# Last mixer: projections of two heads at a time in quarters, with attention units, rotation and head norm of the group ahead of them between

## The reference, cut to what matters

```python
def diff_attn_mixer(h, w_in, lam_vecs, subln_w, w_out, cos, sin, layer):
    y = h @ w_in
    q, k, v = jnp.split(y, 3, axis=-1)
    q = apply_rope(q.reshape(B, L, DIFF_HEADS, 2, DIFF_HEAD), cos, sin)
    k = apply_rope(k.reshape(B, L, DIFF_HEADS, 2, DIFF_HEAD), cos, sin)
    v = v.reshape(B, L, DIFF_HEADS, 2 * DIFF_HEAD)
    lam = jnp.exp(jnp.sum(lv[0] * lv[1])) - jnp.exp(jnp.sum(lv[2] * lv[3])) + lam_init
    o = causal_diff_attention(q, k, v, lam)   # (softmax of component 0 - lam * softmax of component 1) @ v
    o = rmsnorm(o, subln_w, SUBLN_EPS) * (1.0 - lam_init)   # within each head
    return o.reshape(B, L, D_MODEL).astype(h.dtype) @ w_out
```

## Time and profile before

| | us |
|---|---|
| median of 3 runs | 1783.93 |
| lowest and highest | 1777.27, 1785.84 |
| the profiled execution | 1785.98 |
| its span | 1784.2 |

### The profile page before, as it was taken

One profiled execution on the slowest core, in us unless ns is written; L12 is line 12 of the kernel. 1 busy time (PEld: TensorE's weight loads), 2 busy tenths in 40 slices (PEclk: granted clock), 3 DMA queues, 4 the chain that ended last, 5 costly groups with the idle time before them and its releaser, 6 DMA issues. The chain is left out here.

```text
span 1784.2 us, 33804 instructions
## 1 busy us (share of the span) xinstructions
PE 1622.2 (91%) x14218; PEld 1542.3 (86%) x14218; DVE 1036.1 (58%) x1581; ACT 739.4 (41%) x1025; POOL 75.8 (4%) x98
## 2 busy tenths in 40 slices
PE   2999989989998889999789997899998979799997
PEld 2999979989997889999688987899998956689997
DVE  6999466887655665444685524544335365655443
ACT  2554344872215444443450103465333434456432
POOL 0121000001100001100000000000000030000000
PEclk7999989999999999999899976999999985799998
DMA  9898545432113546555330002254442510235451
GB/s 352 293 349 342 195 139 195 166 119 90 61 49 112 189 154 247 186 168 188 107 100 27 2 1 78 88 177 157 170 170 103 168 32 1 95 102 185 164 186 48
DMA packets 39195, 256.77 MB, mean 144 GB/s; under 512 B 4259, under 2 KB 5668, under 8 KB 9892
## 3 DMA queue, kind: packets, MB, share of 16 engines
q1 hardware_dynamic: 37492, 251.07, 40.3%
q10 hardware_dynamic: 1584, 3.97, 0.6%
HBM read 251.87 MB, written 3.15 MB: 143 GB/s over the span
## 5 line engine op out<-in xcount | busy, mean ns | idle before, releaser
L454 DVE TENSOR_TENSOR w_lo<-raw,w_hi 128x2048 fp32r<-128x2048 f32 (+2 forms) x203 | 456.6, 2249 | 474.3 <-ACT w_hi L446 473.5
L528 PE MATMUL bank<-x_hi,w_hi 128*128 128x256 f32 (+1 forms) x2096 | 609.3, 291 | 56.6 <-DVE x_lo L677 28.6
L529 PE MATMUL bank<-x_lo,w_hi 128*128 128x256 f32 (+1 forms) x2096 | 600.0, 286 | 0.0
L530 PE MATMUL bank<-x_hi,w_lo 128*128 128x256 f32 (+1 forms) x2096 | 599.5, 286 | 0.0
L446 ACT ACTIVATE w_hi<-raw 128x2048 fp32r<-128x2048 f32 (+2 forms) x203 | 381.6, 1880 | 422.7 <-PE bank L530 399.6
L528 PEld LDWEIGHTS bank<-x_hi,w_hi 128*128 128x128 f32 x2096 | 401.1, 191 | 67.4 <-issue 53.0
L530 PEld LDWEIGHTS bank<-x_hi,w_lo 128*128 128x128 f32 x2096 | 401.9, 192 | 0.0
L529 PEld LDWEIGHTS bank<-x_lo,w_hi 128*128 128x128 f32 x2096 | 400.4, 191 | 1.0 <-issue 0.7
L528 PE MATMUL bank<-mh_hi,w_hi 128*128 128x272 f32 (+1 forms) x512 | 149.0, 291 | 6.5 <-PEq L2666 6.5
L530 PE MATMUL bank<-mh_hi,w_lo 128*128 128x272 f32 (+1 forms) x512 | 147.7, 289 | 0.0
L529 PE MATMUL bank<-mh_lo,w_hi 128*128 128x272 f32 (+1 forms) x512 | 147.0, 287 | 0.0
(11 more groups left out here) (489 smaller groups left out, 2203.5 us busy)
## 6 DMA issues: line engine op xcount, KB each, us to landing
raw<-in_stream SPq DMA_DIRECT2D x227, 1024.0 KB, 4.8
raw<-in_stream SPq DMA_DIRECT2D x8, 768.0 KB, 4.3
gate_store<-stage ACTq DMA_DIRECT2D x8, 256.0 KB, 2.0
raw<-in_stream SPq DMA_DIRECT2D x4, 512.0 KB, 3.8
h<-in_h ACTq DMA_DIRECT2D x1, 1088.0 KB, 8.2
zt<-gate_store SPq DMA_DIRECT2D x1, 1024.0 KB, 6.5
gate<-gate_store SPq DMA_DIRECT2D x1, 1024.0 KB, 8.6
out<-h SPq DMA_DIRECT2D x8, 128.0 KB, 1.9
```

Source lines behind the costliest of these rows:

```text
L454: nc.vector.tensor_tensor(w_lo[:, s_at % 2, 0:kt], raw[:, r_at % RING, 0:kt], w_hi[:, s_at % 2, 0:kt].bitcast(F32), ALU.subtract).then_inc ...
L528: nc.tensor.matmul(out, hi, xh[:, k0 + k, 0:L], start=start, stop=False)
L529: nc.tensor.matmul(out, hi, xl[:, k0 + k, 0:L], start=False, stop=False)
L530: mm = nc.tensor.matmul(out, lo, xh[:, k0 + k, 0:L], start=False, stop=stop)
```

## The change

The twelve slabs of q, k and v are ordered by groups of two heads: q, k, v of heads 0 and 1, then of 2 and 3, and so on, each slab a section of its own. Blocks 1 to 5 become one block, whose engines walk 26 slots (s from -4 to 21). In slots -4 to 11 PE issues three quarters of a slab in each (a quarter is one half of the columns over four of the eight tiles), so that four slots project a group. Unit s of the attention is issued in slot s, its transposition in s+2, its product with the values in s+3, its head's norm from slot 2h+4 for head h on. While group g is projected, the units of the group before are at work. The last four units have no projections beside them.

The projections accumulate in banks 0 and 1; scores have one pair of banks (2, 3) up to unit 12, the rotation and the transposed values banks 4 and 5, transposed weights bank 6, products with values bank 7. DVE now makes both products of the rotation from the accumulation banks, ahead of the permutation (`turn_products`), and adds the permuted one behind it (`turned`); GpSimd has no part in it. A finished head is copied by ACT. Results of the norm go to `o_hi` and `o_lo` of their own. The block opens with the norm `before_attention`; DVE has ahead of it the first operations for lambda, and SP has `turning` and `lam_row` ahead of the slabs.

```diff
-    add("od_q", 4, by_cols("od_w_in_2", K8), taker="act")
-    add("od_kv", 8, by_cols("od_w_in_2", K8, 0, D), taker="act")
+    for g in range(4):
+        add(f"od_q{g}", 1, by_cols("od_w_in_2", K8, 0, g * SLAB_N))
+        add(f"od_k{g}", 1, by_cols("od_w_in_2", K8, 0, D + g * SLAB_N))
+        add(f"od_v{g}", 1, by_cols("od_w_in_2", K8, 0, 2 * D + g * SLAB_N), taker="act")
...
-        plain(S["od_q"], x_hi[:, :, META:T2], x_lo[:, :, META:T2], q_at, before=before_attention, L=T1)
-        plain(S["od_kv"], x_hi, x_lo, yq)
...
+        GROUPS, UNITS, STREAMED = 4, 2 * HEADS, 12
+        units = [(head, qt) for head in range(HEADS) for qt in range(2)]
+        woven = [S[f"od_{x}{g}"] for g in range(GROUPS) for x in "qkv"] + [S["od_out"]]
+        slots = range(-4, UNITS + 6)
...
+                sp.dma_start(turning[:], t["turning"]).then_inc(a["turn"], 16)
                 sp.dma_start(lam_row[:], t["od_lambda_2"]).then_inc(a["lam"], 16)
-                sp.dma_start(turning[:], t["turning"]).then_inc(a["turn"], 16)
+                load_to(sp, S["od_out"].r0 + 1 + RING)
...
+                def quarter(m):
+                    p, j, k0 = m // 4, m // 2 % 2, 4 * (m % 2)
+                    sec, _, (r, r_at, s, s_at, _) = slab(p)
+                    cols = kept(p % 3)
+                    if m % 4 == 0:
+                        pe.wait_ge(raw_used, r + 1 + RING)
+                        if p == 0:
+                            keep_busy(w_hi[:, s_at % 2, 0, 0:P], w_hi[:, s_at % 2, 1], FIRST_BUSY)
+                    if k0 == 0 and p:
+                        if j:
+                            taken(pe, woven[p - 1], None, 0, 0)
+                        else:
+                            pe.wait_ge(a["half_took"], p)
+                    out = banks[j][:, 0:T2 - cols.start]
+                    for k in range(k0, k0 + 4):
+                        if p == 0 and j == 0:
+                            before_attention.wait_tile(pe, k)
+                        hi = w_hi[:, s_at % 2, k, j * P:(j + 1) * P]
+                        lo = w_lo[:, s_at % 2, k, j * P:(j + 1) * P]
+                        nc.tensor.matmul(out, hi, x_hi[:, k, cols], start=k == 0, stop=False)
+                        nc.tensor.matmul(out, hi, x_lo[:, k, cols], start=False, stop=False)
+                        mm = nc.tensor.matmul(out, lo, x_hi[:, k, cols], start=False, stop=k == 7)
+                    if k0:
+                        mm.then_inc(slab_done if j else a["half_done"], 1)
...
+                def rotated(g, kind):
+                    if g == 0 and kind == 0:
+                        pe.wait_ge(a["turn"], 16)
+                    if kind:
+                        pe.wait_ge(a["rope"], 4 * g + 2)
+                    elif g:
+                        pe.wait_ge(a["v_out"], 2 * g)
+                    n = T2 - kept(kind).start
+                    for j in range(2):
+                        pe.wait_ge(a["by_sin"], 4 * g + 2 * kind + j + 1)
+                        nc.tensor.matmul(banks[4 + j][:, 0:n], rotate, by_sin[:, kind, j, 0:n], start=True, stop=True).then_inc(a["rot"], 1)
+
+                def rows_of_values(g):
+                    half_took = 3 * g + 3
+                    pe.wait_ge(a["rope"], 4 * g + 4)
...
+                def scores(n):
+                    head, qt, C, K = dims(n)
+                    if qt == 0 and head % 2 == 0:
+                        pe.wait_ge(a["rope"], 2 * head + 4)
+                    if n:
+                        pe.wait_ge(u_["exp"], n if n <= STREAMED else n - 1)
+                    if n == STREAMED + 1:
+                        pe.wait_ge(a["v_out"], 2 * GROUPS)
...
+                for s in slots:
+                    first, i, g = 3 * (s + 4), s % 4, s // 4 + 1
+                    if s < STREAMED:
+                        quarter(first)
+                    if 0 <= s < UNITS:
+                        scores(s)
+                    if s >= 5 and s % 2 and (s - 5) // 2 < HEADS:
+                        head_sum((s - 5) // 2)
+                    if s < STREAMED:
+                        quarter(first + 1)
+                    if 0 <= s - 2 < UNITS:
+                        transposed_weights(s - 2)
+                    if s < STREAMED:
+                        quarter(first + 2)
+                    if 0 <= s - 3 < UNITS:
+                        weighted_values(s - 3)
+                    if s < STREAMED and i in (2, 3):
+                        rotated(g, i - 2)
+                    if i == 0 and 0 <= s <= STREAMED:
+                        rows_of_values(s // 4)
...
+                def turn_products(g, kind, j):
+                    p = 3 * g + kind
+                    half_ready(dve, p, j)
+                    if g == 0 and kind == 0 and j == 0:
+                        dve.wait_ge(a["turn"], 16)
+                    if g:
+                        dve.wait_ge(a["rot"], 4 * (g - 1) + 2 * kind + j + 1)
+                    cols = kept(kind)
+                    n = T2 - cols.start
+                    nc.vector.tensor_tensor(by_sin[:, kind, j, 0:n], banks[j][:, 0:n], sin_t[:, cols], ALU.mult).then_inc(a["by_sin"], 1)
+                    nc.vector.tensor_tensor(target(g, kind, j), banks[j][:, 0:n], cos_t[:, cols], ALU.mult).then_inc(dve_took if j else a["half_took"], 1)
...
+                dve.wait_ge(a["lam"], 16)
+                link(dve, "dve", nc.vector.tensor_tensor(lam_p[:], lam_row[:, 0:4:2], lam_row[:, 1:4:2], ALU.mult))
+                nc.vector.reduce_sum(lam_s[:, 0:2], lam_p[:], AX.X).then_inc(a["lam_x"], 1)
+                link(dve, "dve", nc.vector.tensor_scalar(sub_w[:], col("od_subln_w_2", 0), 1.0 - LAM_INIT, None, ALU.mult))
+                before_attention.on_dve(dve, mid_od)
+                split_lo(dve, slab(1))
+                dve.wait_ge(a["lam_e"], 1)
+                link(dve, "dve", nc.vector.tensor_tensor(lam_s[:, 2:3], lam_s[:, 1:2], lam_s[:, 0:1], ALU.subtract))
+                nc.vector.tensor_scalar(lam_s[:, 3:4], lam_s[:, 2:3], -LAM_INIT, None, ALU.add).then_inc(a["lam_x"], 1)
+                for s in slots:
+                    i, g = s % 4, s // 4 + 1
+                    if i == 0 and 0 <= s <= STREAMED:
+                        turned(s // 4, 1)
+                    if s == 0:
+                        dve.wait_ge(a["lam_mm"], 1)
+                        link(dve, "dve", nc.vector.tensor_copy(lam[:], banks[6][:, 0:1]))
+                    if s < STREAMED:
+                        if i == 2:
+                            turn_products(g, 1, 0)
+                        if i == 3:
+                            turned(g, 0)
+                    unit(s)
+                    if s >= 5 and s % 2 and (s - 5) // 2 < HEADS:
+                        mean_square((s - 5) // 2)
+                    if s < STREAMED:
+                        if i == 0:
+                            turn_products(g, 0, 0)
+                        if i == 1:
+                            turn_products(g, 0, 1)
+                        if i == 2:
+                            turn_products(g, 1, 1)
+                        if i and 3 * g + i + 1 < len(woven):
+                            split_lo(dve, slab(3 * g + i + 1))
+                    if s >= 6 and s % 2 == 0 and (s - 6) // 2 < HEADS:
+                        normed((s - 6) // 2)
+                    if s >= 7 and s % 2 and (s - 7) // 2 < HEADS:
+                        low((s - 7) // 2)
...
+                before_attention.on_act(act, mid_od, lambda: split_hi(act, slab(1)))
+                act.wait_ge(a["lam_x"], 1)
+                nc.scalar.activation(lam_s[:, 0:2], lam_s[:, 0:2], ACT.Exp).then_inc(a["lam_e"], 1)
+                for s in slots:
+                    i, g = s % 4, s // 4 + 1
+                    if i == 1 and 1 <= s <= STREAMED + 1:
+                        value_rows(s // 4)
+                    if 0 <= s < UNITS:
+                        exponentials(s)
+                    if s < STREAMED and i == 3:
+                        copy_values(g, 0)
+                    if 0 <= s - 2 < UNITS:
+                        tr_copy(s - 2)
+                    if s < STREAMED and i in (1, 2):
+                        split_next(3 * g + i - 1)
+                    if s >= 4 and s % 2 == 0 and (s - 4) // 2 < HEADS:
+                        head_out((s - 4) // 2)
+                    if s >= 5 and s % 2 and (s - 5) // 2 < HEADS:
+                        root((s - 5) // 2)
+                    if s >= 7 and s % 2 and (s - 7) // 2 < HEADS:
+                        high((s - 7) // 2)
+                    if s < STREAMED and i == 3:
+                        copy_values(g, 1)
+                        split_next(3 * g + 2)
```

More of the change, by code:

```diff
@@ L2649, in mixer_out @@
                 norm, then = Norm(out, L, g_row(layer, 1), add_to=hs), Norm(hs, L, g_row(layer, 2))
-                plain(sec, x_hi, x_lo, out, norm=norm, then=then, L=L)
+                plain(sec, xh, xl, out, norm=norm, then=then, L=L)
             return then
```

(47 more changed lines are left out.)

285 lines of the change are left out of this document (107 added, 178 removed).

## The result

The changed kernel takes 1773.51 us (median of 10 runs, 1772.27 to 1779.31) against 1781.72 for the kernel before in the same comparison (10 runs, 1777.27 to 1785.84). The medians lie 8.2 us apart. The ratio on record is 0.9944, 95% interval 0.9931 to 0.9957, which is some 10 us faster, 7.7 to 12.3.

A forecast was written before the change was run, and what follows sets the result against it. It took 98.5 us without projections as what could be won, and the DVE-ACT split chain as the new limit. Steps of 172.6 us plus 4 gave 176.6 against 179.1, so 1781.4 us; range 1758 to 1797.

The forecast's parts named there:

- 1 opening: Block start to end of first slab: 12.2 us before, plus 3.5 us waiting for lambda behind the tables; 15.7 us.
- 2 two slabs, rotation: After the first slab: two more slabs and one rotation without units, at PE's pace; 13.0 us.
- 3 to scores 1: Value copy, splits, rotated keys, first scores, then PE's list without a unit to finish; 11.7 us.
- 4 scores 1 to 5: First group with units: four slots without norm, root, high and low parts; 33.2 us.
- 5 scores 5 to 9: Second group with units: as a full group of four slots, without one low part; 38.1 us.
- 6 scores 9 to 13: Third group: slot 11 has no split, slot 12 runs at half clock; 32.2 us.
- 7 the rest: Units 13 to 15, then the last unit's attention, its product and the last two heads' norm; 28.7 us.
- The hand-overs: Waits spread over some 80 hand-overs between engines in the block, 0.05 us each; 4 us added.
- PE's own pace: PE's work for a full group at full clock: 28.9 us, 7.2 a slot, against 9.6 expected from the chain.
- A looser chain: Streamed groups near PE's pace, 29 to 33 us each; whole time 1762 to 1774, about 1768; chance 0.35.
- The clock stays at half: PE's waits in the streamed part keep its clock at half; 1826 if throughout, 1797 if partly; chance 0.15.
- Table switches that cost twice their load: Each ScalarE table switch costs another 1.3 us beyond its load; 7 us more, 1788; chance 0.05.

The follow-up runs named there:

- lam_later: Changed kernel with lambda's DMA ahead of the tables' and its DVE operations behind the opening norm; block 167.15 us, 0.9969 of before.
- fill_waits: Changed kernel with useless matmuls on PE ahead of the scores of slots 0, 4, 8 and 12; block 164.73 us, 0.9922 of before.
- splits_slot12: splits_lam with root and high part of the head norm ahead of value copies and high split in slots 3 and 7; block 145.66 us, 1755.16 us.
- splits_slot13: splits_lam with ScalarE's high split of slots 2, 6 and 10 back behind the exponentials; block 151.31 us, 0.9850 of before.
- high_split_first: Changed kernel with ScalarE's high splits ahead of exponentials, or of weight copies, root and high part in fourth slots; block 160.25 us, 0.9891 of before.
- splits_lam: splits_both with lambda's operations also behind the opening norm; block 148.74 us, 0.9830 of before.
- splits_both: Changed kernel with high splits first on ScalarE and each fourth slot's low split behind the next slot's first unit; block 151.56 us, 0.9835 of before.

## Why the prediction came out as it did

The mechanism was right, and so were most terms; one term was added on top that the steps didn't need. Step by step, forecast and measured in the profile of after (the measured steps hold their hand-overs):

| step | forecast us | measured us |
|---|---|---|
| 1 opening | 15.7 | 15.3 (1351.09 to 1366.35) |
| 2 two slabs, rotation | 13.0 | 13.0 |
| 3 to scores 1 | 11.7 | 13.3 |
| 4 scores 1 to 5 | 33.2 | 32.6 |
| 5 scores 5 to 9 | 38.1 | 37.8 |
| 6 scores 9 to 13 | 32.2 | 30.6 |
| 7 the rest | 28.7 | 27.6 |
| hand-overs | 4 | in the steps |
| sum | 176.6 | 170.2 |

- **The hand-overs (4 us) are the step that failed.** I added 80 times 0.05 us to the steps. The price of a unit was read from one start to another start (1478.26 to 1480.90) and held its hand-overs already. The other terms of the chain were mostly durations of single instructions, and in the trace of after these overlap on the same engine by more than the hand-overs take:

```profile
1427.88 0.56 ACT L3051 ACTIVATE attn_tr<-bank 128x128 f32<-128x128 f32 x3
...
1428.35 1.90 ACT L448 ACTIVATE w_hi<-raw 128x2048 fp32r<-128x2048 f32 x1
...
1430.28 2.29 DVE L456 TENSOR_TENSOR w_lo<-raw,w_hi 128x2048 fp32r<-128x2048 f32 x1 [2.06 <-ACT w_hi L448]
...
1432.49 0.43 DVE L2912 TENSOR_TENSOR by_sin<-bank,turning 128x272 f32<-128x272 f32 x1
```

  The split starts 0.09 us before the copy ends and the product 0.08 before the low split ends, against 0.03 us of hand-over from ACT to DVE. From the mask at 1425.23 to this product it is 7.26 us, forecast 2.64 + 0.56 + 1.92 + 2.29 = 7.41. Without the hand-overs the sum is 172.6, 6.5 us faster than before, against 8.9 measured.
- **Opening.** Right in mechanism and size: the norm starts 3.1 us after the block (1354.21), forecast 3.5, and waits for lambda behind the tables. lam_later gives the 3.0 us back.
- **Step 3, 1.6 us short.** The term holds no half clock behind PE's wait. The wait was only 2.47 us, and the clock was at half all the same (0.52 from 1387 to 1390). fill_waits gives back 1.5 us in just this step.
- **Groups 1 and 2.** Within 0.6 us, and by the mechanism named: low splits wait for high splits (27.2 us in 11 places), PE waits 3.84 and 5.14 us at the scores of slots 4 and 8, and the clock is at half behind. I had put these waits at 5 us or more, which only the second is. The slots themselves: masks of units 5 to 9 lie 8.0, 9.1, 11.9 and 8.8 us apart, forecast 7.4 (7.8 without the low part), 9.5, 11.4 and 9.8. The errors, +0.6, -0.4, +0.5 and -1.0, cancel nearly in the sum, which is luck.
- **Group 3 and the rest**, 1.6 and 1.1 us too high. Before the scores of slot 12 PE waited only 2.27 us, and 12 table loads lie in the block, not 16: one for lambda, six for the roots, as the last three roots have no exponentials between them and share one, and five for the exponentials.
- **PE's own pace.** I put a full group of PE's work at 28.9 us. In splits_slot12, where nothing else holds it up, PE is busy for 28.89 us of a second group of 29.4. So the total of PE's list was right. The 8.4 us between this group's 29.4 and after's 37.8 are what the order costs, the half clock included. "PE waits a third of the time" was wrong by its own numbers: 38.5 less 28.9 is a quarter of 38.5, and in the trace PE was idle for 6.5 of 37.8 us.
- **The rivals.** A looser chain, with groups at 29 to 33 us, wasn't the case: 37.8 in the second. That the whole time lies inside its 1762 to 1774 is chance. The clock stays at half: no, it is back at 1.00 by 1390, 1421 and 1459, some 5 to 6 us after PE's work began again at 1384.80, 1416.14 and 1453.31. Table switches that cost twice their load: no, 4.4 us in sum without eleven of them. The Trainium skill (ScalarE: Activation LUTs, What ACT_TABLE_LOAD costs) adds a drain of about 1.38 us to each load; in this case's rows the root starts 0.01 us behind the load's end (1445.80 + 1.28 to 1447.09), and the measurement decides.
- **The chances.** I gave 0.36 to faster by over 0.5%. With the hand-overs left out the same sum would have stood at 1777.4, still within 0.5%; the last 2.4 us were errors of single terms, with both signs.

## What to carry to other kernels

A duration read from start to start already holds the hand-over; before adding hand-overs to durations of single instructions, look in the rows whether the instructions overlap. When work of several chains is put into one order, look in each engine's list for the instruction that waits for another engine and has something more urgent behind it: here one low split of each group, moved behind the next unit's work, was worth 15.7 us, more than the whole change. A wait of PE costs its own length and can cost a while at half clock behind it; here it was two thirds and one third. When two versions differ by one or two us, look at the clock of both before naming the order as the cause: of splits_slot13's 2.1 us some 1.6 were half clock.

## What the runs showed of the hardware

- The clock fell to half after a pause of only 2.47 us. PE stood still until 1384.80, then worked at full clock (1.00 from 1384 to 1386), and ran at 0.52 from 1387 to 1390, although it was busy for all of that time: its projection matmuls start 0.12 us apart up to 1386.42 and 0.21 apart from there. Here the fall comes behind the pause, when work has begun again, and so it does at slot 4 (pause 3.84 us, 0.53 from 1417). At slot 8 (pause 5.14 us) it comes within the pause. With the first pause filled by matmuls, 1.5 us of the step go.
- The length of the pause alone doesn't tell whether the clock falls. Behind a pause of 2.16 us at slot 4 of high_split_first it was 0.50 (1420 to 1422), and behind 2.79 us at slot 8 of the same kernel too (1454 to 1456); behind the same 2.79 us at slot 8 of splits_lam and splits_both it stayed at 1.00. What decides between them stays open.
- A table load took its 1.28 us and no more: the activation behind it starts 0.01 us after its end. Where ACT waits anyway, the load lies in the wait: after the load at 1432.00 the exponential starts only at 1434.68, when DVE has its scale ready. 11 loads fewer made the block 4.4 us shorter, a third of their 14.1 us.
- The rest of the span, with the same code, differed between executions by some 7 us (1600.6 to 1607.8), nearly as much as the change won. Below such a difference the block's own length is the better measure.
